# Latent tails in one block and three blocks, with the expert rows re-staged around them

## The reference

```
o = token_mixer(modulate(x, norm1_g, sh1, sc1), ...)       # conv, retention, mLSTM, window attention
    # merge: acc = sum_i sigmoid(gates[i]) * (ys[i] @ w_branch[i]);  o = acc @ w_out
x = x + ga1 * o
h = modulate(x, norm2_g, sh2, sc2)                          # RMSNorm, gain, scale and shift
q = h @ wq                                                  # (tokens, 8 heads x 2 x 128)
s = q . keys; top 16 of each half, top 16 of the 256 sums   # 128 experts per token
gate = softmax(cv);  act = gelu(h . u[expert])
x = x + ga2 * sum_k gate_k * act_k * v[expert_k]            # rows gathered from tables of 16384 x 1024
```

## Time and profile before

| what | value |
|---|---|
| runs (3), median | 6093.1 us |
| profiled execution | 6088.19 us, span 6086.3 us, mean granted clock 0.763 |
| PE busy | 4101.5 us (67%) |
| DVE busy | 3226.0 us (53%) |
| POOL busy | 2754.4 us (45%) |
| ACT busy | 702.4 us (12%) |
| gathers (queue q0) | 1384.49 MB, 60.1% of 16 engines |
| loads and stores of SP (q1) | 304.03 MB, 16.0% |

### The profile page before, as it was taken

One profiled execution on the slowest core, in us unless ns is written; L12 is line 12 of the kernel. 1 busy time (PEld: TensorE's weight loads), 2 busy tenths in 40 slices (PEclk: granted clock), 3 DMA queues, 4 the chain that ended last, 5 costly groups with the idle time before them and its releaser, 6 DMA issues. The chain is left out here.

```text
span 6086.3 us, 64932 instructions
## 1 busy us (share of the span) xinstructions
PE 4101.5 (67%) x23632; PEld 2449.2 (40%) x23632; DVE 3226.0 (53%) x7722; ACT 702.4 (12%) x1562; POOL 2754.4 (45%) x2606
## 2 busy tenths in 40 slices
PE   5889676668998885554454569898878633334447
PEld 4767544335566663221021125457767500000001
DVE  3522698657434875756544217443268665664430
ACT  1221112123111001000000011233100100000000
POOL 0000144566330445777777730000014477777775
PEclk9999787779999987665555679999989855555555
DMA  6655466899885899999999961112559899999999
GB/s 224 207 164 179 156 234 227 303 322 335 275 293 188 311 331 332 386 363 402 384 400 409 404 269 51 52 46 73 161 190 333 322 379 364 395 378 397 409 402 380
DMA packets 721230, 1739.23 MB, mean 286 GB/s; under 512 B 88912, under 2 KB 371408, under 8 KB 719248
## 3 DMA queue, kind: packets, MB, share of 16 engines
q0 software_dynamic: 380032, 1384.49, 60.1%
q1 hardware_dynamic: 314896, 304.03, 16.0%
q10 hardware_dynamic: 25984, 46.56, 2.2%
HBM read 1706.98 MB, written 27.89 MB: 285 GB/s over the span
## 5 line engine op out<-in xcount | busy, mean ns | idle before, releaser
L3009 POOL DMA_INDIRECT arena<-in_peer_u,arena x1280 | 1408.2, 1100 | 2259.4 <-DVE arena L2107 1093.7
L1275 PE MATMUL bank<-arena 128*32 128x256 f32 x10240 | 1199.9, 563 | 1348.5 <-DMA arena<-in_peer_v,arena 1339.7
L2197 DVE CUSTOM_DVE_ANT_0 arena<-arena 128x1024 f32<-128x1024 f32 x1280 | 1540.6, 1222 | 908.6 <-DMA arena<-in_peer_u,arena 885.6
L3009 POOL DMA_INDIRECT arena<-in_peer_v,arena x1280 | 1319.4, 1031 | 627.7 <-issue 310.9
L1275 PEld LDWEIGHTS bank<-arena 128*32 128x32 f32 x10240 | 252.0, 131 | 2250.6 <-DMA arena<-in_peer_v,arena 2135.9
L784 PE MATMUL bank<-arena 128*128 128x512 f32 (+1 forms) x1856 | 731.6, 550 | 27.9 <-issue 13.1
L1182 PE MATMUL bank<-arena 128*128 128x256 f32 x2560 | 620.3, 398 | 89.0 <-issue 56.2
L1182 PEld LDWEIGHTS bank<-arena 128*128 128x128 f32 x2560 | 506.8, 200 | 184.7 <-issue 99.6
L784 PEld LDWEIGHTS bank<-arena 128*128 128x128 f32 x1856 | 372.8, 206 | 338.2 <-issue 315.0
L1188 PE MATMUL bank<-arena 128*128 128x256 f32 x1280 | 306.6, 382 | 2.3 <-ACT arena L2736 2.3
L1236 PE MATMUL bank<-arena 128*128 128x256 f32 x1280 | 290.1, 390 | 17.8 <-issue 17.8
(11 more groups left out here) (269 smaller groups left out, 3844.5 us busy)
## 6 DMA issues: line engine op xcount, KB each, us to landing
arena<-in_w_in SPq DMA_DIRECT2D x152, 1024.0 KB, 6.9
arena<-in_mod_w POOLq DMA_DIRECT2D x20, 2048.0 KB, 11.5
arena<-in_peer_wq SPq DMA_DIRECT2D x40, 1024.0 KB, 5.5
arena<-in_w_branch SPq DMA_DIRECT2D x60, 512.0 KB
arena<-in_w_out SPq DMA_DIRECT2D x20, 1024.0 KB, 6.8
arena<-in_peer_u,arena POOLq DMA_INDIRECT x1280
arena<-in_peer_v,arena POOLq DMA_INDIRECT x1280
arena<-in_w_branch SPq DMA_DIRECT2D x40, 256.0 KB
```

The lines of the kernel that those rows point to most:

```text
L1275: i = mm(banks[6 + g // 2][32 * j:32 * j + 32, (g % 2) * W:(g % 2 + 1) * W], G["ws"][:, g, 32 * m:32 * m + 32], G["row"][ROW_BUFFER["v", i ...
L2197: v.tensor_tensor_reduce(u, u, G["h2"][it % 2], 1.0, 0.0, ALU.mult, ALU.add, G["dots"][:, n:n + 1]).then_inc(*pr.step("dot", it, n))
L3009: fl.done(eng.indirect_dma_start(G["row"][x], None, table, bass.IndirectOffsetOnAxis(ids[:, n:n + 1], 0)), f"row_landed{x}", (kind + "_lan ...
```

## The change

Latent tails are split into one block and three (c0 stays as it was). All widths of the tail follow, so a merge matmul has 128 columns in the first part and 384 in the second, and `w_out` matmuls go block by block as before. Expert rounds are listed by one function for all engines: the first block's u rows stand beside the second part; its v rows come after that, 32 beside four routing steps of the second block, the other 96 beside the second block's u rows, three for every four. The second block's keys are searched in the second query stage. SP fetches part of the out rows before the merge ends.

```diff
 def halves_of(p):
-    return [(x, x + 1) for x in range(0, p.n // P, 2)]
+    return [(0,), tuple(range(1, p.n // P))] if p.t0 else [tuple(range(p.n // P))]
...
+ROUTE = 4
+V_LEAD = SLOTS // 4
+def led(call):
+    return (call.first,) if call is PC0 else (call.first, call.first + 1)
+def peer_steps(call):
+    first, last, steps = call.first, call.first + len(call.blocks) - 1, []
+    for s in range(ROUTE):
+        steps.append(((first, s), None, None))
+    for n in range(SLOTS):
+        steps.append((None, (first, n), None))
+    if call is not PC0:
+        for n in range(V_LEAD):
+            s, now = divmod(n, V_LEAD // ROUTE)
+            steps.append((None if now else (first + 1, s), None, (first, n)))
+        for n in range(SLOTS):
+            v, now = divmod(n, 4)
+            steps.append((None, (first + 1, n), (first, V_LEAD + 3 * v + now) if now < 3 else None))
+    for it in range(led(call)[-1] + 1, last + 2):
+        for n in range(SLOTS):
+            steps.append((None, (it, n) if it <= last else None, (it - 1, n)))
+    return steps
...
     # row buffers (gather_tables): 8 shared while the first block's u rows and first 32 v rows come, then
+                u_ring = (0, 1, 2, 3, 8, 9, 10, 11)
+                v_ring = range(14) if v and v[0] == last else (4, 5, 6, 7, 12, 13)
...
 def query_units(p, f):       # the part's first block is scored among the chunks, in both parts
+        if c % 4 == 1 and c > 4:
+            order.append(("score", lead, c // 4 - 1))
+    order.append(("score", lead, 3))
+    return order + [("score", x, g) for x in others for g in range(4)]
...
             def merge_part(p, f, part):
+                pn, half, n = p.name, span(p, f), width(p, f)
-                            i = mm(b[:, 0:W], wg[:, k, m * P:(m + 1) * P], HTk(p)[:, k, half], ...)
+                            i = mm(b[:, 0:n], wg[:, k, m * P:(m + 1) * P], HTk(p)[:, k, half], ...)
-                        yield 3.4
+                        yield n / W * 3.4
...
             def outp(p, f):      # vector
-                if f == 0:
-                    eng.wait_ge(*at("out_rows", pn))
-                    v.scalar_tensor_tensor(SC2, SC2, 1.0, G2, ALU.add, ALU.mult)
+                eng.wait_ge(*at("out_gate", pn, f))
...
+                    if y == 0:    # after the first block's residual additions
+                        eng.wait_ge(*at("out_rows", pn, f))
+                        v.scalar_tensor_tensor(T["sc2"], T["sc2"], 1.0, T["g2"], ALU.add, ALU.mult)
...
-            side_by_side("c1", mixer(C1), side, 3 * SLOTS, 1.0)
+            side_by_side("c1", mixer(C1), side, V_LEAD + 3 * SLOTS, 1.0)
...
             # sync: behind the load of the last branch weights of a merge
+            def out_rows_early(p, f):
+                for e in ENG:
+                    eng.wait_ge(*at("end", e, ended))          # the stage before the merge
+                eng.wait_ge(*at("mod_stored", p.l, 1))
+                eng.wait_ge(*at("experts", first_it if f else first_it - 1))
+                dma(T["ga"], mod_piece(p, 2), "out_gate", ("out_gate", p.name, f))
+                residual_in(p, f, halves_of(p)[f][0])
+                dma(T["g2"], norm_row(p), "out_rows")
+                if f == 0:
+                    dma(T["sc2"], mod_piece(p, 4), "out_rows")
+                    dma(T["sh2"], mod_piece(p, 3), "out_rows", ("out_rows", p.name, f))
             # behind the load of the last out weights: waits for the merge's end on all engines
+            def out_rows_late(p, f):
+                if p is C0 or f:
+                    dma(T["sc2"], mod_piece(p, 4), "out_rows")
+                    dma(T["sh2"], mod_piece(p, 3), "out_rows", ("out_rows", p.name, f))
+                for x in halves_of(p)[f][1:] if p.t0 else ():
+                    residual_in(p, f, x)
```

More of the change, by code:

```diff
@@ L115, in gather_tables @@
     for call in (PC0, PL0, PL1):
[L116 to L123, removed]
-            else:
[L125 to L131, removed]
+        last, reader, given = call.first + len(call.blocks) - 1, {}, {"u": 0, "v": 0}
+        for _, u, v in peer_steps(call):
+            if call is PC0:
+                u_ring = range(8) if u and u[0] == call.first else (0, 1, 2, 3)
+                v_ring = (4, 5, 6, 7) if u else range(8)
+            elif u and u[0] == call.first or v and v[0] == call.first and v[1] < V_LEAD:
+                u_ring, v_ring = range(8), range(8)
+            else:
+                u_ring = (0, 1, 2, 3, 8, 9, 10, 11)
+                v_ring = range(14) if v and v[0] == last else (4, 5, 6, 7, 12, 13)
+            for kind, row, ring, step in (("u", u, u_ring, "dot"), ("v", v, v_ring, "v_summed")):
+                if row:
+                    x = ring[given[kind] % len(ring)]
+                    given[kind] += 1
+                    buffer[(kind,) + row], before[(kind,) + row] = x, reader.get(x)
+                    reader[x] = (step,) + row
     return buffer, before
 ROW_BUFFER, READ_BEFORE = gather_tables()
-ROUTE = 4
 CONST = {}
@@ new lines, in peer @@
+                for lead, u, v in peer_steps(call):
+                    if lead:
+                        it, s = lead
+                        if s == 0 and it > call.first:
+                            rows_in(it)
+                        if s == 2:
+                            gate_exp(pr, G, it)
+                    if u:
+                        it, n = u
+                        h, k = divmod(n, TOPK)
+                        if k == TOPK - 1:
+                            gelu(it, h)
+                        if it + 1 <= last and it + 1 not in led(call):
+                            if n == (HEADS - 2) * TOPK:
+                                gate_exp(pr, G, it + 1)
+                            if n == 0:
+                                scores_in(it + 1)
+                            if n == 4:
+                                rows_in(it + 1)
+                        if n == SLOTS - 1:
+                            spread(it)
+                    if v:
+                        it, n = v
+                        if n == 2 and it > call.first:
+                            x_out(it - 1)
+                        if n == 24:
+                            x_in(it)
+                    yield 0
@@ L2998, in gathers @@
                 G = peer_work(call)
-                last = call.first + len(call.blocks) - 1
                 def gather(kind, it, n):
@@ L3118, in _ @@
                     rows_in(starts[name])
-                if name[0] == "out" and name[3] == (D // W - 1 if name[2] == 0 else 0):
-                    out_rows([p for p in PASSES if p.name == name[1]][0], name[2])
+                if name[0] in ("branch", "out"):
+                    p = [p for p in PASSES if p.name == name[1]][0]
+                    if p is not C0 and name[0] == "branch" and name[3:] == merge_parts(p, name[2])[-1][-1]:
+                        out_rows_early(p, name[2])
+                    if name[0] == "out" and name[3] == D // W - 1:
+                        out_rows_late(p, name[2])
             for e in ENG:
```

382 lines of the change are left out of this document (190 added, 192 removed).

## The result

The changed kernel takes 6178.5 us (median of 4 runs, 6172.0 to 6185.2) against 6090.8 (6084.0 to 6100.7) for the kernel before, run beside it: ratio 1.0143, 95% interval 1.0124 to 1.0162. It is slower, by 1.4%. The forecast was 6081, the range ended at 6150, and slower had a chance of 0.29. The spans of the two profiled executions differ by 87.0 us (6173.3 and 6086.3), as the medians do (87.6).

The account below looks back on a forecast made before the run. Row gathers at the DMA's limit alone bound 4843 to 6080 us; the tails ahead left it room. Layer 0 -70 + 92 - 13 = +9, layer 1 -100 + 92 - 13 = -21, together -12: 6081 us, range 6000 to 6150.

Parts of the forecast that it names:

- Layer 0, first part: Layer 0's one-block part: merges and the stretch ahead net 45 us saved (10 to 75); with out and query 70.
- 38 lost: Layer 0 from 700 to 1562 us: 66 us of moved gathers land partly in idle DMA time, costing 38 us.
- Some 48 value rows: Gathers that the planner moves ahead of layer 0's merges at 1562 us: 66 us of DMA, 40 of TensorE.
- The first rival: Weight stream bounds the first parts: layer 0 saves 10 and not 45, total 6144 us; chance 0.22.
- 13 gained: Gather phase behind each second part: eight prefetched value rows save 11 us, the restart 2 (5 to 18).
- TensorE's prices at the two new widths: Matmul instructions in the merges: 0.111 us each at 128 columns, 0.324 at 384.
- layer 1's first part: Layer 1's one-block merges, out and query: 100 us saved (57 to 108).
- both second parts: Three-block merges, out and query of each layer: +92 us (+75 to +105).
- The load stays hidden at 128 columns: Merges at 128 columns cost 0.111 us an instruction; the rival, load not hidden, had 0.164, total 6142, chance 0.07.
- 4 us a stage and not 13: Layer 1's first out stage and the way to the query: early row fetch and one block save 13 us (8 to 15).
- The sum of out and query: First part's out and query stages: 25 us saved in each layer, in layer 1 as 13 and 12.
- the 25 us of dots and 49 of search: Second query stage: VectorE's dots and copies 25 us and four head pairs 49, within 115 in all, +42.

Follow-up runs that it names:

- a_pace: Changed kernel with its first part's yields costed as at the old width of 256 columns, so context steps are handed out almost as slowly as before: 6165.5 us, 1.0130.
- d_nosearch: Changed kernel with the second block's key search left out of the second query stage (part of the computation missing): 6146.9 us, 1.0089.
- m_free_ring: Changed kernel with the rings of the paired stretch begun at buffers that the rows alone did not use: 6153.9 us, 1.0097.
- i_late_rows: Changed kernel with all out rows fetched only when the merge has ended, on the chip with slower gathers: 6355.4 us, 1.0085.
- l_share1_again: Kernel before with the context's expert steps spread over 100% and not 90% of layer 0's pass: 6072.1 us, 0.9979.
- o_mended: f_pace_share1 with the rings of m_free_ring: 6130.6 us, 1.0064 against the kernel before.
- f_pace_share1: a_pace with the context's steps spread over the whole pass and not 90%, on the chip with slower gathers: 6331.1 us, 1.0044.
- e_before_share1: Kernel before with layer 0's context steps spread over 100% and not 90% of the pass, on the chip with slower gathers: 6291.4 us, 0.9974.
- h: Changed kernel with 64 instead of 32 of the first block's value rows ahead of the second block's u rows, slower chip: 6342.4 us, 1.0062.

## Why the prediction failed

**The step that failed is "Layer 0, first part": net 45 saved, where 14 were lost** in the stretch ahead of the merges and the merges together, 59 of the 99 us by which the sum was off. Within it the term "38 lost" measured 94; the merges saved 80 where 83 were forecast. The direction of the move was seen, its price was not. "Some 48 value rows" was a good count: 50 more gathers lie ahead of the first gate matmul (467 against 417), all of them value rows. But I priced them where they end up, at 1.38 us each with a part falling into idle DMA. The faster pace acts earlier. Windows up to the same point of the main work and from there to the first gate matmul, and PE's waits for value rows in the first of them; before, then after:

```profile
700.00:1362.00 662.00, 450.71 (x1974) 262.61 (x1972) 487.61 (x1220) 129.61 (x261) 331.28 (x294) 0.78 0.76 264
1362.00:1583.00 221.00, 186.29 (x1564) 111.45 (x1564) 123.15 (x255) 70.64 (x170) 125.73 (x123) 0.96 0.91 321
...
PE bank L1275 <- DMA arena<-in_peer_v,arena: 76.1, 39, 5.2
```

```profile
700.00:1460.00 760.00, 490.36 (x2259) 274.34 (x2259) 530.73 (x1295) 138.82 (x267) 410.52 (x366) 0.76 0.79 279
1460.00:1677.00 217.00, 186.89 (x1676) 112.30 (x1675) 82.41 (x180) 65.53 (x165) 98.23 (x101) 0.99 0.78 271
...
PE bank L1323 <- DMA arena<-in_peer_v,arena: 127.4, 57, 7.5
```

The same main work ends at 1362 and at 1460. Up to there the change has 72 gathers more, since a step of the second round carries a u and a v row, and takes 98 us more: 1.36 each, nothing hidden. TensorE stands for value rows for 127.4 us instead of 76.1. Behind that point it has 22 gathers fewer and takes only 4 us less: TensorE waits for value rows for 8.3 us there before and for 6.8 after, so there was little to give back. The average share of 0.79 hid this.

The runs split the 59 in another way. At the old pace the split would save 8 here and not 45 (a_pace): 37. The pace adds 22. So the term fails twice: the rows that move cost more, and if they stay the merges do not get shorter by what TensorE saves.

**The first rival was right in its place.** It said that the weight stream keeps layer 0's merges from saving: 10 us. At the old pace (a_pace) they and what lies ahead of them save 8, with 46.8 us of waits for weights. But the rival meant the changed kernel's own pace, at which 14 are lost; that its number fits a_pace is luck. It was wrong for layer 1, whose merges save 70.3 where the forecast had 75 and the rival 47. So its total, 6144, fell short as well.

**Behind the second part.** "13 gained" was wrong in sign, twice, for 43 of the 99 us. Of the eight value rows that were to be prefetched, six were issued before the spread in layer 1 and five in layer 0, three of them (4906.72 to 4909.58) early; the next waited 12.08 us for VectorE's dots, by the order in which u and v rows stand. In layer 1 there follows the wait for a buffer. But d_nosearch had all eight ahead, and m_free_ring lost the wait, and the phases of neither are clearly shorter; so neither explains the time. Means over the single traces at the higher rate: peer1 1278.0 in four traces with the old order (1273.6 to 1285.4), 1288.3 in five with the changed one (1278.6 to 1295.1); peer2 1224.5 (1222.3 to 1226.3) and 1235.1 (1226.8 to 1244.5); with the rings mended 1281.1 and 1280.0, 1225.7 and 1232.2. The wait for a buffer and its end are shown, in layer 1 alone; that it costs time is not. Why the changed order's phases are some 10 us longer on these chips stays open, and so does why peer1 of the changed kernel lost 15.6 and peer2 1.4, since one kernel's own phase varies by 12.

**What held.** TensorE's prices at the two new widths (0.115 and 0.326 us an instruction against 0.111 and 0.324), layer 1's first part (96.6 against 100), both second parts (+91.4, +90.9 against +92), and layer 1's second part window by window. The load stays hidden at 128 columns: the rule of the Trainium skill, TensorE: Matmul & The Clock Gate, section Back-to-back issue gap, would have made it 0.160 as estimated, and the trace says 0.115 in a merge of 768 instructions; so the trace disagrees, for this stream. VectorE no longer waits for rows at layer 1's first out stage; it waits for TensorE:

```profile
4398.44 0.42 DVE L2039 SCALAR_TENSOR_TENSOR arena<-bank,arena 128x256 f32<-128x256 f32 x1 [5.33 <-PE bank L1264]
```

Yet i_late_rows shows that this is worth 4 us a stage and not 13: there VectorE waits 11.7 us for the rows and not 16.8, then finds the matmuls' results ready and adds without a pause. Most of the wait lies beside the out matmuls of the block. The sum of out and query was right, its split was not. In the second query stage the 25 us of dots and 49 of search were added up; leaving the search out gives back 10 to 12 us, so most of it lies beside TensorE's 99 us there.

**What the split is worth without its mishaps.** Its fair partner is l_share1_again, with the same spread of the context's steps (on another chip of the same rate). Against its trace o_mended is 36.5 us ahead at layer 0's second part (1916.9, 1953.4), loses 86.9 there, saves 96.8 in layer 1's first part, loses 92.8 in its second, and 13.1 in the gather phases: 60 with the rest, in two single traces of a split with its pace and its rings mended. The pair on one chip, f_pace_share1 and e_before_share1, is 40 apart in the medians, there with the changed order's shorter peer1. A second part bound by TensorE at 384 columns gains nothing from a lower DMA share, and one block in the first part saves its full TensorE time only where neither weights nor gathers are short, in layer 1.

## What to carry to other kernels

When work is split unevenly, check what the planner makes of the changed costs: steps paced by a share of the cost move with it, and they must be priced where they land. Take the same point of the main work in both kernels and count what has been issued up to it, not only the balance at the end of the stage. A narrower part of a pass pays only where the transfer beside it has room; a wider part pays its full price wherever the engine is the bound. Where the order of transfers changes its pattern, follow the buffers over the seam: the first one of the new pattern may be the last one of the old; then ask whether the wait costs time at all.

## What was not expected of the hardware

The kernels e, f, h and i ran on a chip where full gathers move less. Same stretch, the kernel before (first chip) and e_before_share1 (the other):

```profile
5500.00:5800.00 300.00, 124.34 (x918) 23.56 (x922) 144.62 (x244) 1.91 (x8) 229.56 (x232) 0.50 1.02 403
```

```profile
5500.00:5800.00 300.00, 114.34 (x828) 21.79 (x831) 154.96 (x284) 4.58 (x10) 224.94 (x206) 0.50 0.98 365
```

232 gathers against 206 in 300 us. Layer 1's merge and its out and query stages take the same on both, 270.2 and 120.8; peer1 and peer2 take 1378.0 and 1321.1 us instead of 1276.8 and 1222.3 in the same kernel (l_share1_again). There the changed order's peer1 is shorter (1360.2 to 1365.8), where on the faster chips it is longer. That the ratio of the changed kernel depends on the chip is likely from this but was not measured, as it never ran there unaltered. Within one run the rate varies too: in peer1 of the kernel before it goes from 381 GB/s (2600 to 3000 us) to 406 (3000 to 3400), at shares of 0.99 and 1.03. The cause stays open.
